# Gate matmuls in two passes of 128 columns that add up in PSUM, and an earlier place for several transfers

## The chip, the cores and the metric

One core of a Trainium2 chip runs the whole block in one launch. The metric is the time on the device in microseconds (us), the median of several runs. The kernel before takes 1783.82 us, the median of 3 runs (1779.32 to 1789.91).

## The reference

One decoder block for 512 tokens of width 1024, in float32: adaLN modulation, a mixer (differential attention beside a gated linear recurrence), and then a PEER layer, which the change is about. PEER scores each token in 8 heads against two sets of 128 keys, keeps the best 16 of each, and picks the 16 best sums; a pair (i1, i2) names one of 128 x 128 experts. For the 8 x 16 chosen experts of a token:

```
q = (h @ w_pq).reshape(B, S, PEER_HEADS, 2, PEER_QHALF)
s = jnp.einsum('bshjd,hjnd->bshjn', q, sub_keys)
v1, i1 = lax.top_k(s[..., 0, :], 16);  v2, i2 = lax.top_k(s[..., 1, :], 16)
cand = v1[..., :, None] + v2[..., None, :]
cidx = i1[..., :, None] * 128 + i2[..., None, :]
top_s, pos = lax.top_k(cand.reshape(..., 256), 16)
gate = softmax(top_s)
a = einsum('tkd,td->tk', expert_u[idx], h)
y = einsum('tk,tkd->td', gate * gelu(a), expert_v[idx])
```

## The kernel before, in words

For 384 of the 512 tokens (SD) the kernel computes every expert densely and multiplies by a gate that is zero where the expert was not chosen; for the other 128 tokens (own rows) it gathers the chosen rows of expert_v and the chosen activations with indirect DMAs on GpSimd. The experts stand in 128 units of 128: a unit of `expert_u` is a tile of 128x1024, multiplied by the transposed activations into a bank of 128x512. All such products are made from float32r halves: a tile is split by ScalarE into a high part (`hi`, Copy to float32r) and by VectorE into the low remainder (`low`), and TensorE runs three passes (high x high, high x low, low x high), 24 matmuls of 512 columns a unit.

The stages from the selection on:
- `stage_select` makes the key scores and, beside the sorting on VectorE, the first 28 units.
- `stage_gates` goes in 48 rounds of 8 tokens (ROUND) and makes one unit (`tile`) in each. The gates of a token are a 128x128 matrix (first index by second index). Its stationary operand is a one-hot of the first indices (`first`, float32r); its moving operand is the one-hot of the second indices weighed by the gate (`weighed`). The gate is split in a high and a low part, h = 0 and 1, that lie side by side, so one matmul of 256 columns per token gives both (line 1829). Four tokens (PER) fill a pair of banks, two such chunks (CHUNKS) a round. ScalarE copies the high halves of a chunk into `gates` (`read_high`, line 1743) and VectorE adds the low halves to them (`add_low`, line 1792). TensorE starts a chunk of the next round when `gates_read` tells that it has been read. The order of the work on each engine is written out in the loop of each engine's block; every 4 rounds SyncE stores a buffer of gates (`store_gates`).
- `stage_rest` makes the last 52 units, keeps 28 of them in memory (`kept`), and weighs each with its gates (`weigh`). SyncE's queue begins with the wait for all stores of the stage before (lines 1890 to 1893), loads two groups of gates, and only then goes on with the unit loads; `store` follows each load six units behind (lines 1898 to 1908). RAW = 4 buffers hold raw units.
- `stage_experts` runs 128 tiles of `expert_v` (18 matmuls each) in an order that mixes tiles whose weighed activations are kept, stored, or plain (to be weighed here); SyncE loads `v_raw`, `acts` and, per group of four plain tiles, `group_gates`. GpSimd gathers own rows (`fetch_row`, line 2154, up to six ahead) and own activations (`fetch_act`, line 2160, one chunk of 16 ahead, on two semaphores); VectorE multiplies a chunk of own activations by the gates (`weigh_own`, line 2250) and adds the rows (`add_row`, line 2260) between its other work, from tile 8 on (`first_row`).

## Time and profile before

| | us |
|---|---|
| median of 3 runs | 1783.82 |
| the profiled execution | 1788.98 |
| its span, first to last instruction | 1787.2 |
| TensorE busy | 1708.3 (96%) |
| VectorE busy | 1311.3 (73%) |
| ScalarE busy | 758.6 (42%) |
| GpSimd busy | 524.9 (29%) |

PE is TensorE's matmuls, PEld its weight loads, DVE VectorE, ACT ScalarE, POOL GpSimd, SP SyncE. Busy times are the union of the records, and records of matmuls overlap: what a matmul costs in a stream is the distance between two starts, not its duration. PEclk and "granted clock" are the share of TensorE's full clock (2.4 GHz) that it was given.

### The profile page before, as it was taken

The page shows a single profiled execution, that of the slowest core. Times are in us where ns is not written, and L with a number is a line of the kernel's source. Part 1 is how long each engine was busy: PE and PEld are TensorE (multiplying, and loading weights), DVE is VectorE, ACT ScalarE, POOL GpSimd, SP SyncE. Part 2 cuts the span into 40 slices and gives each one's busy share as a digit, 9 for nine tenths or more (in the row PEclk, how much of TensorE's full clock was granted, in tenths as well). Part 3 has the DMA queues.
Part 4 walks back from the last instruction along what each step waited for, and adds up shares of the span by engine and source line. Part 5 has one row for each costly group of instructions (what it writes and reads, how often), then busy time and mean ns, then how long its engine had stood idle before and what let it go on. Part 6 is the DMA issues. An engine that isn't in the chain of part 4 may idle for free. (4 is left out here: it accounts for less than half of the span.)

```text
span 1787.2 us, 22493 instructions
## 1 busy us (share of the span) xinstructions
PE 1708.3 (96%) x7869; PEld 1411.2 (79%) x7869; DVE 1311.3 (73%) x2200; ACT 758.6 (42%) x1261; POOL 524.9 (29%) x423
## 2 busy tenths in 40 slices
PE   6999896989999999999998999999999999999997
PEld 5877675778877778888886888888788888888786
DVE  5787776559999969999994333333578868787878
ACT  5225344343322367777773222232333333333333
POOL 1000001115667610000000000000767668667750
PEclk9999998989999999999999999999999999999999
DMA  9563001332144435765667665553898999898985
GB/s 381 214 244 108 1 1 43 147 130 80 62 136 141 139 132 171 217 211 190 204 217 247 214 207 183 176 176 110 307 343 308 329 330 335 314 326 322 335 326 224
DMA packets 160415, 369.96 MB, mean 207 GB/s; under 512 B 16608, under 2 KB 78560, under 8 KB 157024
## 3 DMA queue, kind: packets, MB, share of 16 engines
q1 hardware_dynamic: 137824, 302.08, 48.5%
q0 software_dynamic: 22528, 67.19, 10.7%
q8 instruction: 21, 0.34, 0.1%
q14 instruction: 42, 0.34, 0.1%
HBM read 306.30 MB, written 62.91 MB: 207 GB/s over the span
## 5 line engine op out<-in xcount | busy, mean ns | idle before, releaser
L2022 PE MATMUL banks<-hl,actT 128*128 128x512 f32 x2268 | 518.3, 391 | 7.4 <-DVE actT L2244 7.3
L2022 PEld LDWEIGHTS banks<-hl,actT 128*128 128x128 f32 x2268 | 427.3, 189 | 98.1 <-DVE hl L2239 8.9
L1997 PE MATMUL banks<-actT,hl 128*128 128x512 f32 x1224 | 280.1, 391 | 7.0 <-ACT kept_acts L1931 6.7
L2154 POOL DMA_INDIRECT rows<-in_v,own_index x65 | 86.5, 1331 | 675.0 <-POOLq L1856 608.8
L1814 PE MATMUL banks<-actT,hl 128*128 128x512 f32 x1176 | 275.9, 390 | 1.8 <-PEq L1351 1.8
L1997 PEld LDWEIGHTS banks<-actT,hl 128*128 128x128 f32 x1224 | 231.2, 189 | 56.0 <-issue 7.8
L1814 PEld LDWEIGHTS banks<-actT,hl 128*128 128x128 f32 x1176 | 217.7, 188 | 45.3 <-issue 2.2
L2197 ACT ACTIVATE hl<-v_raw 128x1024 fp32r<-128x1024 f32 x125 | 132.4, 1059 | 273.3 <-PE banks L2022 206.9
L1592 PE MATMUL banks<-actT,hl 128*128 128x512 f32 x1032 | 241.5, 392 | 6.3 <-POOL hl L1439 5.0
L1592 PEld LDWEIGHTS banks<-actT,hl 128*128 128x128 f32 x1032 | 191.5, 188 | 49.6 <-POOL hl L1439 5.9
L2239 DVE TENSOR_TENSOR hl<-v_raw,hl 128x1024 fp32r<-128x1024 f32 x125 | 153.2, 1226 | 77.6 <-ACT hl L2197 57.2
L2160 POOL DMA_INDIRECT rowg<-early_activations,own_at x128 | 175.0, 1367 | 39.1 <-issue 39.1
L1732 ACT ACTIVATE gate_hits<-second_hits,gate_parts 128x128 fp32r<-128x128 bf16 x288 | 125.5, 516 | 68.6 <-DVE second_hits L1772 68.6
L1965 DVE TENSOR_TENSOR kept_acts<-kept_acts,group_gates 128x384 f32<-128x384 f32 x52 | 28.8, 558 | 162.6 <-ACT kept_acts L1931 162.6
L1439 POOL TENSOR_TENSOR hl<-raw,hl 128x1024 fp32r<-128x1024 f32 x42 | 116.5, 2775 | 99.6 <-ACT hl L1453 99.6
L1685 DVE TENSOR_TENSOR gate_hits<-second_hits,gate_parts 128x640 fp32r<-128x640 bf16 x96 | 120.6, 1337 | 0.0
L1931 ACT ACTIVATE kept_acts<-banks 128x512 f32<-128x512 f32 x52 | 31.0, 597 | 192.7 <-PE banks L1997 192.7
L2154 POOL DMA_INDIRECT raw<-in_v,own_index x63 | 83.5, 1325 | 55.8 <-DVE raw L2260 21.9
L217 PE MATMUL banks<-actT,hl 128*128 128x512 f32 x384 | 89.8, 397 | 2.9 <-DVE actT L583 2.9
L217 PEld LDWEIGHTS banks<-actT,hl 128*128 128x128 f32 x384 | 73.8, 193 | 18.5 <-issue 2.9
L1956 DVE TENSOR_TENSOR hl<-raw,hl 128x1024 fp32r<-128x1024 f32 x50 | 61.3, 1227 | 36.1 <-ACT hl L1922 36.1
L716 PE MATMUL banks<-hl,actT 128*128 128x512 f32 x288 | 66.5, 391 | 4.1 <-DVE hl L198 4.1
(274 smaller groups left out, 2173.2 us busy)
## 6 DMA issues: line engine op xcount, KB each, us to landing
raw<-in_u SPq DMA_DIRECT2D x128, 512.0 KB, 3.9
v_raw<-in_v SPq DMA_DIRECT2D x128, 512.0 KB
expert_gates<-gates SPq DMA_DIRECT2D x12, 2048.0 KB, 9.8
group_gates<-expert_gates SPq DMA_DIRECT2D x32, 768.0 KB
wada<-in_w_ada SPq DMA_DIRECT2D x10, 2048.0 KB, 8.3
acts_in<-early_activations SPq DMA_DIRECT2D x100, 192.0 KB
early_activations<-kept_acts SPq DMA_DIRECT2D x52, 256.0 KB, 2.2
early_activations<-gate_acts SPq DMA_DIRECT2D x48, 256.0 KB, 2.3
```

The lines of the kernel that those rows point to most:

```text
L217: last = nc.tensor.matmul(bank[:], hl[:, a, u % m.split, kc * P:(kc + 1) * P], m.actT[:, b, kc, :], start=(kc == 0 and j == 0), stop=(kc = ...
L1439: g.tensor_tensor(hl[:, 1, u, :], raw[:, u, :], hl[:, 0, u, :].bitcast(F32), ALU.subtract).then_inc(m.unit_lo, 1)
L1592: last = nc.tensor.matmul(m.psum[u % 2][:], hl[:, x, u % m.split, kc * P:(kc + 1) * P], m.actT[:, z, kc, :], start=(kc == 0 and j == 0), s ...
L1685: return eng.tensor_tensor(weighed[:, buf, lo:hi, h, :].rearrange("p t k -> p k t"), hits[:, buf, :, lo:hi], part[h][:, n].unsqueeze(1).to ...
L1732: last = A(weighed[:, r % BUFS, u, h, :], hits[:, r % BUFS, :, u], ACT.Copy, scale=part[h][:, at:at + 1])
L1814: last = nc.tensor.matmul(m.psum[n % 2][:], hl[:, x, n % m.split, kc * P:(kc + 1) * P], m.actT[:, z, kc, :], start=(kc == 0 and j == 0), s ...
L1997: last = nc.tensor.matmul(m.psum[u % 2][:], hl[:, x, u % m.split, kc * P:(kc + 1) * P], m.actT[:, z, kc, :], start=(kc == 0 and j == 0), s ...
L2022: last = nc.tensor.matmul(bank(m, t, half)[:], w[:, x, t * P:(t + 1) * P], m.hl[:, z, j, half * S:(half + 1) * S], start=(first and k == 0 ...
L2154: nc.gpsimd.indirect_dma_start(out=fetched[k % FETCH], out_offset=None, in_=rows_of_v, in_offset=bass.IndirectOffsetOnAxis(ap=m.own_index[ ...
L2160: nc.gpsimd.indirect_dma_start(out=own_act[:, k:k + 1], out_offset=None, in_=acts_of_u, in_offset=bass.IndirectOffsetOnAxis(ap=m.own_at[:, ...
L2197: A(v[:, 0, j, :], v_raw[:, j, :], ACT.Copy).then_inc(v_hi, 1)
L2239: V.tensor_tensor(v[:, 1, j, :], v_raw[:, j, :], v[:, 0, j, :].bitcast(F32), ALU.subtract).then_inc(v_lo, 1)
```

## The change

Five things change.

1. A token's gates are made by two matmuls of 128 columns with the same stationary operand, the first with the high part (start) and the second with the low part (stop), so that the sum stands in PSUM. A chunk of four tokens fills one bank instead of two. Chunk 0 is copied out by ScalarE and chunk 1 by VectorE, each once, and each has a semaphore of its own; the addition is gone.
2. In `stage_rest` the wait for the stores of the stage before, and the two gates loads behind it, come after two more unit loads. Stores follow eight units behind instead of six (LATE). The loads of four plain activations, and the first gates that `stage_experts` wants, are issued within the loop instead of after it.
3. The first weighings of `stage_rest` are made at unit 5 instead of 3.
4. In `stage_experts` gathers of own activations run further ahead (`ahead(k)`, up to 8 more), over three semaphores instead of two.
5. Own rows are added from tile 12 on instead of tile 8.

```diff
-        def halves(c):
-            return m.pairs[1 + c][:].rearrange("p (t h j) -> p h j t", t=PER, h=2)
+        def tokens(c):
+            return m.psum[2 + c].rearrange("p (t j) -> p j t", t=PER)
@@ stage_gates, scalar
-                for c in range(CHUNKS):
-                    act.wait_ge(gated, r * CHUNKS + c + 1)
-                    at = r % per_half * ROUND + c * PER
-                    A(gates[:, k, :, at:at + PER], halves(c)[:, 0], ACT.Copy).then_inc(high_read, 1)
+                act.wait_ge(gated, r * CHUNKS + 1)
+                at = r % per_half * ROUND
+                A(gates[:, k, :, at:at + PER], tokens(0), ACT.Copy).then_inc(gates_read[0], 1)
@@ stage_gates, vector
-            def add_low(r):
+            def read_second(r):
                 k = r // per_half % 2
-                for c in range(CHUNKS):
-                    dve.wait_ge(high_read, r * CHUNKS + c + 1)
-                    at = r % per_half * ROUND + c * PER
-                    dst = gates[:, k, :, at:at + PER]
-                    V.tensor_tensor(dst, dst, halves(c)[:, 1], ALU.add).then_inc(gates_read, 1)
+                if r >= 2 * per_half and r % per_half == 0:
+                    dve.wait_ge(stored[k], r // (2 * per_half) * 16)
+                dve.wait_ge(gated, (r + 1) * CHUNKS)
+                at = r % per_half * ROUND + PER
+                V.tensor_copy(gates[:, k, :, at:at + PER], tokens(1)).then_inc(gates_read[1], 1)
@@ stage_gates, tensor
-                        pe.wait_ge(gates_read, i * (per_half * CHUNKS) + ((b - 1) * CHUNKS + c + 1))
+                        pe.wait_ge(gates_read[c], i * per_half + b)
                     for k in range(PER):
                         u = c * PER + k
-                        last = nc.tensor.matmul(m.pairs[1 + c][:, k * 2 * NKEY:(k + 1) * 2 * NKEY], first[:, b % BUFS, u, :],
-                                                weighed[:, b % BUFS, u, :, :].rearrange("p h j -> p (h j)"),
-                                                start=True, stop=True)
+                        for h in range(2):
+                            last = nc.tensor.matmul(m.psum[2 + c][:, k * NKEY:(k + 1) * NKEY], first[:, b % BUFS, u, :],
+                                                    weighed[:, b % BUFS, u, h, :], start=(h == 0), stop=(h == 1))
@@ stage_rest, sync
-            for k in range(2):
-                sp.wait_ge(m.stored[k], 16 * GATE_PAIRS)
-            for u in range(RAW):
-                sp.wait_ge(acts_stored[u], 16 * stored_before)
-            load_gates(0)
-            load_gates(1)
-            for u in range(2):
-                sp.wait_ge(m.early_stored[u], 16 * EARLY // 2)
-            for n in range(RAW, count + RAW + 2):
+            for n in range(RAW, count + LATE):
+                if n == RAW + 2:
+                    for k in range(2):
+                        sp.wait_ge(m.stored[k], 16 * GATE_PAIRS)
+                    for u in range(RAW):
+                        sp.wait_ge(acts_stored[u], 16 * stored_before)
+                    load_gates(0)
+                    load_gates(1)
...
-                if n >= RAW + 2:
-                    store(n - RAW - 2)
+                if n >= LATE:
+                    store(n - LATE)
...
+                if n == count - JG:
+                    for j in range(JG):
+                        sp.dma_start(m.acts_in[:, j, :], a.early[TILES[JG + j], :, 0:SD]
+                                     ).then_inc(m.acts_landed[j], 16)
+                if n - LATE == count - JG - 1:
+                    free = (count // JG - 2) % 2
+                    sp.dma_start(gates[:, free].rearrange("p b j t -> p (b j t)"),
+                                 a.gates[:, SEQUENCE[1][0] * size:(SEQUENCE[1][0] + 1) * size]
+                                 ).then_inc(gates_landed[free], 16)
@@ stage_rest, vector
-                if n == 3:
-                    weigh(0)
-                    weigh(1)
-                if n >= 3:
+                if n == CLEAR:
+                    for k in range(CLEAR - 1):
+                        weigh(k)
+                if n >= CLEAR:
                     weigh(n - 1)
@@ stage_experts
-        first_row = 8
+        first_row = 12
...
+            def ahead(k):
+                return min(SLOTS, k + 1 + CHUNK_K + min(FETCH + 2, k // 2))
...
-                    if c < chunks - 1:
-                        fetch_act(k + CHUNK_K)
+                    for q in range(ahead(k - 1) if k else CHUNK_K, ahead(k)):
+                        fetch_act(q)
```

## Rows read from the trace of the kernel before

**Rows 1.** Busy time and share, and the costliest groups, from the page

```profile
PE 1708.3 (96%) x7869; PEld 1411.2 (79%) x7869; DVE 1311.3 (73%) x2200; ACT 758.6 (42%) x1261; POOL 524.9 (29%) x423
...
L1814 PE MATMUL banks<-actT,hl 128*128 128x512 f32 x1176 | 275.9, 390 | 1.8 <-PEq L1351 1.8
```

**Rows 2.** Busy by stretch: length; PE, PEld, DVE, ACT, POOL (instructions); clock, DMA, GB/s

```profile
720.00:760.00 40.00, 40.00 (x200) 33.98 (x200) 40.00 (x44) 31.57 (x64) 0.00 (x0) 1.00 0.68 212
960.00:1000.00 40.00, 33.29 (x138) 27.08 (x137) 11.54 (x15) 10.10 (x13) 0.00 (x0) 0.91 0.74 250
1240.00:1280.00 40.00, 35.84 (x146) 28.82 (x145) 19.08 (x28) 14.24 (x21) 25.07 (x22) 0.91 0.75 277
1600.00:1700.00 100.00, 98.06 (x433) 80.92 (x433) 80.71 (x95) 36.86 (x50) 75.41 (x51) 1.00 0.90 328
```

**Rows 3.** One round in order of time: start, length (us), engine, line

```profile
761.23 1.27 DVE L1792 TENSOR_TENSOR gates<-gates,banks 128x512 f32<-128x512 f32 x2
...
762.87 1.11 PE L1829 MATMUL banks<-gate_hits,first_hits 128*128 128x256 f32 x8
...
763.82 5.63 PE L1814 MATMUL banks<-actT,hl 128*128 128x512 f32 x24
...
765.31 2.51 DVE L1685 TENSOR_TENSOR gate_hits<-second_hits,gate_parts 128x640 fp32r<-128x640 bf16 x2
...
767.66 1.27 DVE L1792 TENSOR_TENSOR gates<-gates,banks 128x512 f32<-128x512 f32 x2
...
769.29 1.11 PE L1829 MATMUL banks<-gate_hits,first_hits 128*128 128x256 f32 x8
```

**Rows 4.** Groups by line: tiles, shapes, count | busy us, mean ns | idle

```profile
L1829 PE MATMUL banks<-gate_hits,first_hits 128*128 128x256 f32 x384 | 53.6, 282 | 0.1
...
L1829 PEld LDWEIGHTS banks<-gate_hits,first_hits 128*128 128x128 f32 x384 | 52.3, 190 | 4.1 <-issue 0.5
L1743 ACT ACTIVATE gates<-banks 128x512 f32<-128x512 f32 x96 | 51.1, 584 | 0.0
...
L233 DVE COPY projT<-banks 128x512 f32<-128x512 f32 x16 | 11.0, 689 | 11.4 <-PE banks L217 11.4
```

**Rows 5.** TensorE in order of time, two short stretches

```profile
33.24 1.84 PE L277 MATMUL banks<-ones,ada_sums 128*128 128x1 f32 x16
...
387.60 1.05 PE L1605 MATMUL banks<-keys,qT 128*128 128x128 f32 x8
```

**Rows 6.** The weight load of the bf16 matmuls, by line

```profile
L1047 PEld LDWEIGHTS banks<-negmask,ident_bf 128*128 128x128 bf16 x32 | 3.0, 95 | 14.0 <-issue 13.1
```

**Rows 7.** Busy by stretch, as rows 2, and TensorE in order of time

```profile
974.00:978.00 4.00, 4.00 (x10) 3.13 (x11) 3.79 (x6) 2.04 (x3) 0.00 (x0) 0.50 0.26 77
...
973.81 6.52 PE L1997 MATMUL banks<-actT,hl 128*128 128x512 f32 x18 [6.71 <-ACT kept_acts L1931]
```

**Rows 8.** SyncE's queue in order of time, entry of the rest stage

```profile
954.05 0.48 SPq L1699 DMA_DIRECT2D expert_gates<-gates  x1
...
965.54 1.00 SPq L1904 DMA_DIRECT2D raw<-in_u  x2
```

**Rows 9.** Waits of TensorE from 950 on: total, times, longest

```profile
PE banks L2022 <- DVE actT L2244: 7.3, 4, 3.2
PE banks L1997 <- ACT kept_acts L1931: 6.7, 1, 6.7
```

**Rows 10.** In order of time, the start of the experts stage

```profile
1247.69 0.33 SPq L2127 DMA_DIRECT2D group_gates<-expert_gates  x1
...
1257.18 0.56 DVE L2232 TENSOR_TENSOR slotsT<-acts_in,group_gates 128x384 f32<-128x384 f32 x1 [6.28 <-DMA group_gates<-expert_gates]
...
1259.49 25.85 PE L2022 MATMUL banks<-hl,actT 128*128 128x512 f32 x101 [3.18 <-DVE actT L2244]
```

**Rows 11.** What line 2250 waited for, and one resumption of TensorE

```profile
  DMA rowg<-early_activations,own_at: 41.3, 8
...
1662.89 3.42 PE L2022 MATMUL banks<-hl,actT 128*128 128x512 f32 x14 [1.94 <-DVE actT L2244]
```

More of the change, by code:

```diff
@@ L1696, in store_gates @@
                 p, k = divmod(q, 2)
-                sp.wait_ge(gates_read, (q + 1) * per_half * CHUNKS)
+                for c in range(CHUNKS):
+                    sp.wait_ge(gates_read[c], (q + 1) * per_half)
                 dst = a.gates[:, 0:NKEY * SD].rearrange("p (g n) -> p g n", n=NTB * JG * TB)
@@ L1734, in scale_rows, with read_first @@
                 last.then_inc(act_rows, 1)
-            def read_high(r):
+            def read_first(r):
                 k = r // per_half % 2
@@ L1748, in _ @@
                     gelu(n - 1)
-                    read_high(n - 1)
+                    read_first(n - 1)
                 hi(n + 2)
@@ L1753, in _ @@
             gelu(count - 1)
-            read_high(count - 1)
+            read_first(count - 1)
         @block.vector
@@ L1797, in _ @@
                 if n >= 1:
-                    add_low(n - 1)
+                    read_second(n - 1)
                 if n + 1 < count:
@@ L1803, in _ @@
                     operands(n + 1)
-            add_low(count - 1)
+            read_second(count - 1)
         @block.tensor
@@ L1849 @@
 CLEAR = 5
+LATE = 8
 MADE = 2
@@ L1888, in store @@
                 sp.dma_start(a.early[WEIGHED_FROM + n], kept[:, n % KEPT, :]).then_inc(acts_stored[n % RAW], 16)
-            for k in range(2):
-                sp.wait_ge(m.stored[k], 16 * GATE_PAIRS)
-            for u in range(RAW):
-                sp.wait_ge(acts_stored[u], 16 * stored_before)
-            load_gates(0)
-            load_gates(1)
-            for u in range(2):
-                sp.wait_ge(m.early_stored[u], 16 * EARLY // 2)
-            for n in range(RAW, count + RAW + 2):
+            for n in range(RAW, count + LATE):
[6 more added lines that the diff above has]
+                    load_gates(1)
+                    for u in range(2):
+                        sp.wait_ge(m.early_stored[u], 16 * EARLY // 2)
                 if n % JG == 1 and 3 <= n // JG < 7:
@@ L1904, in _ @@
                     sp.dma_start(raw[:, n % RAW, :], a.u[WEIGHED_FROM + n]).then_inc(m.unit_landed[n % RAW], 16)
-                if n >= RAW + 2:
-                    store(n - RAW - 2)
+                if n >= LATE:
+                    store(n - LATE)
                 if n % JG == 3 and 2 <= n // JG < count // JG:
                     load_gates(n // JG)
-            for j in range(JG):
-                sp.dma_start(m.acts_in[:, j, :], a.early[TILES[JG + j], :, 0:SD]).then_inc(m.acts_landed[j], 16)
+                if n == count - JG:
[7 more added lines that the diff above has]
+                                 ).then_inc(gates_landed[free], 16)
             for j in range(MADE):
@@ L2071, in stage_experts @@
         fetch_landed = [sem(f"fetch_landed{i}") for i in range(FETCH)]
-        act_landed = [sem("own_act_landed0"), sem("own_act_landed1")]
+        act_landed = [sem(f"own_act_landed{i}") for i in range(3)]
         fetch_read, own_weighed, own_added = sem("fetch_read"), sem("own_weighed"), sem("own_added")
@@ L2093, in loads_before, with gate_buffer @@
             return sum(k != "kept" for k in kinds[:n // JG])
+        def gate_buffer(q):
+            return (rest_groups + q) % 2
         def source(n):
@@ L2123, in load_gates @@
                 q = plain_before(s * JG) // JG
+                b = gate_buffer(q)
                 if q >= 2:
@@ L2126, in load_gates @@
                 at = SEQUENCE[s][0] * size
-                sp.dma_start(gates[:, q % 2].rearrange("p b j t -> p (b j t)"), a.gates[:, at:at + size]
-                             ).then_inc(gates_landed[q % 2], 16)
+                sp.dma_start(gates[:, b].rearrange("p b j t -> p (b j t)"), a.gates[:, at:at + size]
+                             ).then_inc(gates_landed[b], 16)
             for s in range(GROUPS + 1):
-                if s < GROUPS and kinds[s] == "plain":
+                if 2 <= s < GROUPS and kinds[s] == "plain":
                     load_gates(s)
@@ L2226, in weigh @@
                 q = i // JG
+                b = gate_buffer(q)
                 if j == 0:
-                    dve.wait_ge(gates_landed[q % 2], ((rest_groups + 1 - q % 2) // 2 + q // 2 + 1) * 16)
+                    dve.wait_ge(gates_landed[b], ((rest_groups + 1 - b) // 2 + q // 2 + 1) * 16)
                 dve.wait_ge(acts_landed[j], (loads_before(n) + 1) * 16)
@@ L2232, in weigh @@
                 V.tensor_tensor(weighed[:, i % 3, :].rearrange("p (b t) -> p b t", t=TB),
-                                acts[:, j, :].rearrange("p (b t) -> p b t", t=TB), gates[:, q % 2, :, j, :],
+                                acts[:, j, :].rearrange("p (b t) -> p b t", t=TB), gates[:, b, :, j, :],
                                 ALU.mult).then_inc(weighed_done, 1)
```

6 lines of the change are left out of this document (3 added, 3 removed).

## The prediction

> **What bounds the kernel now.** I read the page's busy times first: TensorE has work for 96% of the span, VectorE 73%, ScalarE 42% [rows 1]. So a change pays only where it shortens TensorE's queue or closes one of its holes. Then the busy times by stretch: in the gates stage (about 647 to 955 us) TensorE and VectorE are both busy for 40.00 of 40 us at full granted clock; around 960 to 1000 and 1240 to 1280 TensorE has holes and a granted clock of 0.91 [rows 2].
>
> Two engines at 100% leave open which one sets the pace, so I took one round of the stage in order of time. TensorE's small matmuls start at 762.87, the unit's big ones at 763.82, the next small ones at 769.29 [rows 3]. So 8 matmuls of 256 columns take 0.95 us (0.119 each), a unit's 24 of 512 columns 5.47 us (0.228 each), a round 6.42 us. From the record of the 24 themselves, less the length of one, 0.39 [rows 1], (5.63 - 0.39) / 23 = 0.228: the pitch inside a unit is that of the whole, so nothing is waited for between unit and round. VectorE's round (761.23 to 767.66) is 6.43 us: it is just as full, but its results are early: the two additions end at 762.50, before the small matmuls that overwrite their banks, and the operands of a round are made in the round before (they end at 767.82; matmuls at 769.29). ScalarE has air: it is busy 31.57 of the 40 us [rows 2]. TensorE sets the pace, with VectorE on its heels.
>
> **The gates part: what goes.** Per round of 8 tokens ScalarE read two high halves, 128x512 each, 51.1 us / 96 = 0.53 us; VectorE added two low halves, 1.27 us together [rows 3, 4]. Now ScalarE copies one 128x512 chunk and VectorE the other. An existing VectorE copy of that shape from PSUM takes 0.69 us [rows 4], so VectorE sheds about 0.6 us a round and ScalarE 0.5, 29 and 25 us in all. I price both at nothing: TensorE ran back to back and waits for neither. Were VectorE the pace-setter by a hair, TensorE's own pitch, 0.227 in a later stage (433 in 98.06 busy us [rows 2]), allows with 24 x 0.227 + 8 x 0.119 = 6.40 us at most 0.02 a round, 1 us in the stage.
>
> **What comes.** A token had one matmul of 256 columns (high and low side by side) and gets two of 128 with the same stationary operand, so per round 16 instead of 8, in the stage 768 instead of 384, and each comes with a weight load of its own: in the trace there are as many loads as matmuls, 384 and 384 [rows 4]. The stream of columns is the same, 2048 a round; the loads double. So the question is the pitch of an fp32r matmul of 128 columns, which the trace of before doesn't show. Bounds:
> - Below: columns alone. 512 columns take 0.227 us and 256 take 0.119, which is 0.108 for 256 columns and some 0.012 fixed; 128 would be 0.066 us. 16 x 0.066 = 1.06 us a round against 0.95: +0.1 us, +5 us in the stage.
> - Above: that a narrow fp32r matmul falls back to what plain fp32 costs. The plain key matmuls of 128 columns are recorded as two each, 8 records in 1.05 us [rows 5]; less the length of a short matmul's record, 0.28 [rows 4], that is 0.77 / 7 = 0.110 a record, so 0.220 us a matmul. 16 x 0.220 = 3.52: +2.57 us a round, +123 us.
> - Between: the weight load sets it. Matmuls of a single column against f32 weights, 16 in 1.84 us, have a pitch of (1.84 - 0.28) / 15 = 0.104 us [rows 5], hardly less than at 128 columns. So a float32 load can't be followed by the next in less than about 0.104 to 0.110 us, however few columns stream. That the fp32r load is no quicker is in its record: 190 ns mean [rows 4], where a bf16 load takes 95 [rows 6].
>
> I take 0.120 us, today's pitch at 256 columns, where the columns (0.107) and the load (0.104 to 0.110) are about equal: the nearest row of the same type and weights. A round then costs 16 x 0.120 - 0.95 = +0.97 us, and 48 rounds **+46.5 us**. With 0.110 it is 48 x 0.81 = +39.
>
> The Trainium skill ("TensorE: Matmul & The Clock Gate", "LDWEIGHTS") says a load takes its columns divided by 1.2, 107 ns for 128; the single-column row (0.104) agrees, and by it alone the stage would grow by 48 x (1.71 - 0.95) = 36 us. The same page's isolated gap, N/2.4 + 2.5 ns ("Back-to-back issue gap"), would make 56 ns of 128 columns and the stage 3 us shorter; the single-column row speaks against it for float32 weights.
>
> Waits that this part changes: TensorE now waits per chunk for the engine that copies it. ScalarE copies chunk 0 behind the GELU, VectorE chunk 1 behind the operands of the round before, and both have a whole unit (5.5 us) for it. Behind ScalarE's copy stand the next split and its rows, behind VectorE's the hits, a subtraction and operands, 6.4 - 0.6 = 5.8 us in a round that now lasts 7.4; the slack grows everywhere. VectorE's new wait for the stored buffer is ScalarE's of before.
>
> **The late order of transfers.** This part closes holes. Each is its idle time plus what the halved clock after it costs (granted 0.50 at 974 to 978, that is 1.2 GHz, 10 matmuls in 4 us [rows 7]).
> - Entry of the rest stage. SyncE issues the last gates store at 954.05, waits for it, and only then issues the next unit loads at 965.54 [rows 8]; they keep ScalarE waiting, and its GELU keeps TensorE idle 6.7 us [rows 9]. Then 18 matmuls take 6.52 us [rows 7], where 17 x 0.227 + 0.39 = 4.25: 2.3 us. Now loads 4 and 5 are issued ahead of the wait (their buffers are free by then), and TensorE has units 3 to 5, over 16 us, to cover the store and load 6. What is late next is load 6, queued behind the store and both gates loads: landed by about 973, its unit starts at about 983. Gain 9.0 us.
> - Start of the experts. SyncE issues the first gates load at 1247.69, VectorE gets it at 1257.18 after 6.3 us, and TensorE stands 3.2 us; then 101 matmuls take 25.85 us [rows 10] against 100 x 0.227 + 0.39 = 23.1: 2.8 us. Now that load and four of activations go out within the rest stage. On SyncE's queue they pass in front of the last unit stores, which move back by two steps, and GpSimd's first gathers wait for those; gain 5.9 us (3.18 + 2.75). Deferring four weighings to CLEAR is covered: TensorE waits for no weighing there.
> - In the experts VectorE waits 41.3 us in eight places for the gathered own activations [rows 11], and three of them reach TensorE: 7.3 - 3.2 = 4.1 us [rows 9] (the last of the three is in [rows 11]). The gathers now run up to 8 ahead. GpSimd issues as many as before, only earlier, so its total doesn't grow. The first row is added at tile 12 instead of 8: 128 rows in 116 tiles instead of 120, 3% denser, where VectorE with all its work is busy 80.7 of 100 us [rows 2]: it fits. If it doesn't, the end of the stage shows it.
> Sum 9.0 + 5.9 + 4.1 = 19.0. I expect nine tenths, **-17 us**; at worst it is 0 or costs a few us, DMA being busy 0.75 to 0.9 of the time there.
>
> **Sum.** 1788.98 (the profiled execution; its span is 1787.2) + 46.5 - 17 = 1818.5. The profiled execution lies 5.2 us above the median of the three runs, 1783.82; beside that median the sum is 1813. Forecast: **1813 us, +1.6%**, slower.
>
> **Rivals.**
> 1. *Fallback to the plain fp32 price* (0.220 us). For it: the trace has no fp32r matmul under 256 columns, and all 128-column ones are plain and cost that. Against: the type stays fp32r, and at 256 it streams a column per cycle. Then 1783.8 + 123 - 17 = 1890 us.
> 2. *The load is hidden* (0.066 us). For it: 512 and 256 columns lie on a line, and the second pass has the same weights as the first. Against: the single-column pitch. Then 1783.8 + 5 - 17 = 1772 us, faster. It decides from a pitch of about 0.082 us down, where 48 x (16 p - 0.95) is the 17 us that the late order gives back.
> 3. *The load price, but the late order returns nothing*: the loads moved forward collide with stores and gathers, or own rows in fewer tiles run into the end. For it: DMA shares of 0.75 and 0.74 in the stretches of the two large holes [rows 2]. Then 1783.8 + 46.5 and 0 to 5 more: 1830 to 1835 us.
> 4. *Nothing moves*: a pitch near 0.082 with the late order as forecast, 1784. No row lies there.
>
> **Chances.** Forecast 0.73 (1800 to 1826: 0.110 with the whole 19 is 1804, 0.120 with half of it 1821, the rest is the spread of runs); rival 1 0.14; rival 2 0.05; rival 3 0.06; rival 4 0.02. The range 1798 to 1838 holds the forecast and rival 3, 0.79. What a measurement can tell from no change is about 0.5%, 9 us. Faster: rival 2 and a little, 0.06; same: rival 4 and the low edge, 0.05; slower 0.89.
>
> **What would show it.** Right: 768 records of the gate matmuls at a pitch near 0.12 us, a round of about 7.4 us, VectorE with 1.5 us idle in each, no idle time of TensorE at the entry of the rest stage nor at the start of the experts, granted clock 1.00 in both stretches, no long wait of VectorE for gathered activations. Wrong: 0.07 or 0.22 us of pitch (or two records per pass); a TensorE wait for a chunk's copy; the same holes as before.

## The result and the profile after

The changed kernel takes 1812.74 us, the median of 4 runs (1809.01 to 1817.06), beside 1784.28 us of the kernel before (1779.32 to 1789.91); the measured ratio is 1.014, 95% interval 1.0112 to 1.0167 (the two medians give 1.016). That is slower, by an amount clear of the spread. Its profiled execution has 1809.01 us and a span of 1807.3.

In the gates stage TensorE still runs back to back, and now no other engine does. One round in order of time (start, length, engine, line), against [rows 3]:

```profile
763.39 1.90 PE L1830 MATMUL banks<-gate_hits,first_hits 128*128 128x128 f32 x16
...
765.13 5.71 PE L1814 MATMUL banks<-actT,hl 128*128 128x512 f32 x24
765.39 0.69 DVE L1792 COPY gates<-banks 128x512 f32<-128x512 f32 x1 [1.43 <-PE banks L1830]
...
770.68 1.90 PE L1830 MATMUL banks<-gate_hits,first_hits 128*128 128x128 f32 x16
...
772.61 0.69 DVE L1792 COPY gates<-banks 128x512 f32<-128x512 f32 x1 [1.28 <-PE banks L1830]
```

The 16 narrow matmuls run from 763.39 to 765.13: 1.74 us, 0.109 each, where 8 wide ones took 0.95. The unit's 24 take 5.55 us (765.13 to 770.68) instead of 5.47. The round has grown from 6.42 to 7.29 us (763.39 to 770.68). VectorE, packed before, now stands 1.3 to 1.4 us in each round until the banks are ready. The groups by line, against [rows 4]:

```profile
L1830 PEld LDWEIGHTS banks<-gate_hits,first_hits 128*128 128x128 f32 x768 | 93.0, 191 | 4.1 <-issue 0.5
L1830 PE MATMUL banks<-gate_hits,first_hits 128*128 128x128 f32 x768 | 91.2, 272 | 0.1
...
L1792 DVE COPY gates<-banks 128x512 f32<-128x512 f32 x48 | 33.1, 690 | 64.7 <-PE banks L1830 64.7
...
L1743 ACT ACTIVATE gates<-banks 128x512 f32<-128x512 f32 x48 | 28.7, 597 | 12.1 <-PE banks L1830 12.1
```

Twice the loads of the same mean length (191 ns), half the columns each, and one copy for each of two engines: 33.1 us of VectorE in place of 61.4, 28.7 of ScalarE in place of 51.1. In this stage it bought no time; behind it, it did (see "Looking for the fastest").

Behind the gates stage the holes have closed. TensorE's waits from 945 us on, all of them, against [rows 9]:

```profile
PE banks L2031 <- PEq L1857: 0.5, 1, 0.5
PE banks L2006 <- PEq L1651: 0.3, 1, 0.3
```

and the stretches of [rows 2], with 1000 to 1040 and 1280 to 1320, since the stage borders now come 30 to 40 us later (length, busy of PE, PEld, DVE, ACT, POOL, then the clock):

```profile
720.00:760.00 40.00, 40.00 (x225) 34.62 (x224) 31.92 (x34) 26.42 (x50) 0.00 (x0) 1.00 0.65 197
960.00:1000.00 40.00, 39.68 (x215) 33.86 (x214) 22.95 (x24) 20.09 (x35) 0.00 (x0) 1.00 0.70 216
1000.00:1040.00 40.00, 40.00 (x179) 33.10 (x178) 14.45 (x17) 11.88 (x15) 0.00 (x0) 1.00 0.77 273
1240.00:1280.00 40.00, 39.53 (x175) 32.46 (x174) 12.11 (x15) 11.57 (x17) 0.08 (x1) 1.00 0.26 91
1280.00:1320.00 40.00, 40.00 (x178) 33.06 (x178) 22.21 (x30) 15.75 (x22) 26.94 (x23) 1.00 0.71 263
1600.00:1700.00 100.00, 100.00 (x443) 82.81 (x442) 82.06 (x96) 35.76 (x50) 70.20 (x55) 1.00 0.94 339
```

The clock is 1.00 in each, late in the kernel TensorE is busy for 100.00 of 100 us, and the gathered activations are never waited for; line 2267, which waited 41.3 us before [rows 11], has no wait listed. SyncE's queue at the entry of the rest stage shows why, against [rows 8]:

```profile
991.98 0.37 SPq L1700 DMA_DIRECT2D expert_gates<-gates  x1
997.01 3.42 SPq L1906 DMA_DIRECT2D raw<-in_u  x2
1001.69 0.80 SPq L1884 DMA_DIRECT2D group_gates<-expert_gates  x2
```

Two unit loads stand between the last gates store (991.98) and the end of its wait (1001.69). How the span divides:

| | gates stage, first to last small matmul | from there to the end of the span |
|---|---|---|
| before | 302.6 | 837.3 |
| after | 344.2 | 816.4 |
| difference | +41.6 | -20.9 |

### The profile page after: what moved, and what is told of

Read it like the earlier page. It is cut to its first block and busy times, and to the rows that moved or that the text cites. A ratio compares the mean times of both kernels' runs of the same rounds, so it can differ in the third digit from the quotient of the medians.

```text
span 1807.3 us, 23187 instructions
## 1 busy us (share of the span) xinstructions
PE 1743.7 (96%) x8253; PEld 1447.2 (80%) x8253; DVE 1289.7 (71%) x2152; ACT 744.3 (41%) x1213; POOL 502.6 (28%) x423
## 5 line engine op out<-in xcount | busy, mean ns | idle before, releaser
L2031 PE MATMUL banks<-hl,actT 128*128 128x512 f32 x2268 | 514.2, 389 | 0.0
L2167 POOL DMA_INDIRECT rows<-in_v,own_index x65 | 76.4, 1176 | 715.4 <-POOLq L1857 640.8
L1974 DVE TENSOR_TENSOR kept_acts<-kept_acts,group_gates 128x384 f32<-128x384 f32 x52 | 28.7, 557 | 156.8 <-ACT kept_acts L1940 156.8
L1685 DVE TENSOR_TENSOR gate_hits<-second_hits,gate_parts 128x640 fp32r<-128x640 bf16 x96 | 118.3, 1313 | 0.0
L1830 PEld LDWEIGHTS banks<-gate_hits,first_hits 128*128 128x128 f32 x768 | 93.0, 191 | 4.1 <-issue 0.5
L1830 PE MATMUL banks<-gate_hits,first_hits 128*128 128x128 f32 x768 | 91.2, 272 | 0.1
L2167 POOL DMA_INDIRECT raw<-in_v,own_index x63 | 74.3, 1179 | 58.2 <-DVE raw L2277 33.6
```

Source lines behind the costliest of these rows:

```text
L1685: return eng.tensor_tensor(weighed[:, buf, lo:hi, h, :].rearrange("p t k -> p k t"), hits[:, buf, :, lo:hi], part[h][:, n].unsqueeze(1).to ...
L1830: last = nc.tensor.matmul(m.psum[2 + c][:, k * NKEY:(k + 1) * NKEY], first[:, b % BUFS, u, :], weighed[:, b % BUFS, u, h, :], start=(h == ...
L2031: last = nc.tensor.matmul(bank(m, t, half)[:], w[:, x, t * P:(t + 1) * P], m.hl[:, z, j, half * S:(half + 1) * S], start=(first and k == 0 ...
L2167: nc.gpsimd.indirect_dma_start(out=fetched[k % FETCH], out_offset=None, in_=rows_of_v, in_offset=bass.IndirectOffsetOnAxis(ap=m.own_index[ ...
```

## The experiments

The runs were timed in three groups, each side by side with the kernel before: `gates_alone`, `late_alone`, `narrow64` and `twice256` (median of the kernel before 1785.4 us); `high_only`, `bf16_two`, `entry_back` and `gathers_back` (1787.2); the other four (1783.8). Between groups ratios are compared, not medians. "Gates stage" is the time from the first to the last small matmul of the profiled execution.

### Each half of the change by itself

`gates_alone` is the kernel before with the new `stage_gates`; `late_alone` is the changed kernel with the old one, its reads and additions included:

```diff
@@ late_alone, against the changed kernel, stage_gates
-                        for h in range(2):
-                            last = nc.tensor.matmul(m.psum[2 + c][:, k * NKEY:(k + 1) * NKEY], first[:, b % BUFS, u, :],
-                                                    weighed[:, b % BUFS, u, h, :], start=(h == 0), stop=(h == 1))
+                        last = nc.tensor.matmul(m.pairs[1 + c][:, k * 2 * NKEY:(k + 1) * 2 * NKEY], first[:, b % BUFS, u, :],
+                                                weighed[:, b % BUFS, u, :, :].rearrange("p h j -> p (h j)"),
+                                                start=True, stop=True)
...
```

> The kernel before with the gates part alone: two passes of 128 columns, one copy per chunk; all transfers in the old order. Theory (the weight load sets the pitch of the narrow matmuls, and the two parts of the change are independent): a round of the gates stage lasts 7.28 us as in the changed kernel, 48 rounds x 0.86 = +41 us, and the three kinds of holes (rest entry, start of the experts, gathers) stay: 1784 + 41 = 1825 us, ratio 1.023. Rival (the longer gates stage itself takes away part of the holes, since stores have more time): under 1818 us, and the entry hole of 6.7 us is smaller in the profile.

> The changed kernel with the gates part undone: one matmul of 256 columns per token, read by ScalarE and added by VectorE as before, with the late order of transfers. Theory: no idle time of TensorE after 950 but the two stage borders, 1784 - 20 = 1764 us, ratio 0.989; gates rounds of 6.42 us. Rival (the late order closes the holes only because the longer gates stage gives its stores time): a hole of several us stays at the entry of the rest stage and the time is 1770 or more.

| | median, us | ratio, 95% | gates stage | from there to the end |
|---|---|---|---|---|
| gates_alone | 1819.54 | 1.0174 (1.0122 to 1.0225) | 344.1 | 823.0 |
| late_alone | 1771.95 | 0.9922 (0.9892 to 0.9952) | 302.6 | 817.9 |

The gates stage is what the small matmuls make it, whatever the order of transfers: 302.6 or 344.1. But the two halves aren't independent. `gates_alone` came out at 1819.5, not 1825: beside the new gates part the old order loses less. `late_alone` came out at 1772, not 1764; a hole of 1.3 us stays, less than the "several us" of the rival that forecast 1770 or more, and most of the miss lies in the size of the holes, taken up below. The waits of TensorE in `gates_alone`, and then those of `late_alone`:

```profile
PE banks L2022 <- DVE actT L2244: 2.7, 2, 2.2
PE banks L1997 <- ACT kept_acts L1931: 2.5, 1, 2.5
```

```profile
PE banks L2006 <- ACT kept_acts L1940: 1.3, 1, 1.3
```

In `gates_alone` the hole at the entry is 2.5 us instead of 6.7 [rows 9], and the granted clock stays at 1.00 from 1012 to 1024, so the 2.3 us of half clock are gone too. In the experts stage TensorE waits 2.7 us instead of 7.3, 2.2 of them at the start, and there too the clock stays at 1.00 (1298 to 1310), where the prediction had counted 2.8 us for it. That is 4.2 + 2.3 + 4.6 + 2.8 = 13.9 of the 14.3 us between 837.3 and 823.0. VectorE still waits 38.6 us for gathered activations, in eight places, but only 0.6 of it reaches TensorE instead of 4.1; why was not followed up. For the entry SyncE's queue tells more:

```profile
988.50 5.81 SPq L1705 DMA_DIRECT2D raw<-in_u  x1
...
996.80 0.37 SPq L1700 DMA_DIRECT2D expert_gates<-gates  x1
...
1007.31 1.67 SPq L1904 DMA_DIRECT2D raw<-in_u  x3
```

and that of the kernel before, ahead of what [rows 8] shows of it:

```profile
946.88 5.83 SPq L1704 DMA_DIRECT2D raw<-in_u  x1
```

In `gates_alone` the last small matmul starts at 995.7 and the last gates store is issued at 996.80, 1.1 us later. Before, it was 949.9 and 954.05, 4.2 us later [rows 8]: SyncE was still held up by a unit load whose issue takes 5.83 us behind the store of 2 MB ahead of it. In `gates_alone` that hold-up (988.50 to 994.3) is over as the last round begins (994.10). So the unit loads behind the wait go out 11.6 us after the last small matmul (1007.31) instead of 15.6 (965.54).

The rival named for `gates_alone` gets its smaller hole, though not its time (under 1818). Its reason, the longer stage, is not the whole of it: `high_only` and `bf16_rows` below keep rounds of 6.4 us and shift SyncE's queue just as far.

### What a narrow matmul costs

```diff
@@ narrow64, against the changed kernel
-                            last = nc.tensor.matmul(m.psum[2 + c][:, k * NKEY:(k + 1) * NKEY], first[:, b % BUFS, u, :],
-                                                    weighed[:, b % BUFS, u, h, :], start=(h == 0), stop=(h == 1))
+                            at = k * NKEY + h * (NKEY // 2)
+                            last = nc.tensor.matmul(m.psum[2 + c][:, at:at + NKEY // 2], first[:, b % BUFS, u, :],
+                                                    weighed[:, b % BUFS, u, 0, h * (NKEY // 2):(h + 1) * (NKEY // 2)],
+                                                    start=True, stop=True)
@@ twice256, against late_alone
+                        for again in range(2):
+                            last = nc.tensor.matmul(m.pairs[1 + c][:, k * 2 * NKEY:(k + 1) * 2 * NKEY],
...
@@ high_only, against the changed kernel
-                        for h in range(2):
+                        for h in range(1):
...
-                                                    weighed[:, b % BUFS, u, h, :], start=(h == 0), stop=(h == 1))
+                                                    weighed[:, b % BUFS, u, h, :], start=True, stop=True)
```

> The changed kernel with each of the 16 gate matmuls of a round cut to 64 columns (the two of a token give the left and the right half of the high part; the low part of the gates is left out). Theory (the float32 weight load sets the pitch): 0.111 us each as at 128 columns, a round 7.28 us, the time that of the changed kernel, 1813 us within 0.3%. Rival (an fp32r pass narrower than 256 columns streams at half rate, two cycles a column): 64 columns take 0.053 + 0.006 = 0.06 us, 16 of them 0.95 instead of 1.8 us, the time 1813 - 41 = 1772 us.

> The kernel with the late order alone, each gate matmul of 256 columns issued twice (the same result written again): 16 loads and 4096 columns a round instead of 8 and 2048. Theory (a load costs about 0.11 us and hides behind 256 columns at best equally long): pitch 0.119 to 0.120 us, a round 6.42 + 0.96 = 7.38 us, 46 us more than the late order alone, that is 5 us slower than the changed kernel though it streams twice its columns: 1810 us. Rival (columns are what costs): the same as the theory gives for this one, but narrow64 then is fast. If VectorE's round of 6.4 us and the bank reads got in the way, the round would be over 7.5 us with waits of TensorE for gates_read.

> The changed kernel without the second pass: 8 fp32r matmuls of 128 columns a round (the low part of the gates is left out). Theory (cost = number of loads x 0.111 us): the small matmuls of a round take 0.89 us, as long as 8 of 256 columns (0.95), a round 6.36 us and the time 3 to 4 us under the late order alone: 1768 us. Rival (the accumulation in PSUM by the second pass is what costs, or the wait for a chunk's copy): then 8 of 128 columns would have a pitch of 0.066 us and a round of 6.0 us: 1752 us.

The small matmuls and the unit after them, in `narrow64`, `twice256` and `high_only`:

```profile
760.53 5.71 PE L1814 MATMUL banks<-actT,hl 128*128 128x512 f32 x24
766.08 1.87 PE L1831 MATMUL banks<-gate_hits,first_hits 128*128 128x64 f32 x16
767.78 5.71 PE L1814 MATMUL banks<-actT,hl 128*128 128x512 f32 x24
```

```profile
765.07 2.08 PE L1830 MATMUL banks<-gate_hits,first_hits 128*128 128x256 f32 x16
766.98 5.63 PE L1814 MATMUL banks<-actT,hl 128*128 128x512 f32 x24
772.45 2.08 PE L1830 MATMUL banks<-gate_hits,first_hits 128*128 128x256 f32 x16
```

```profile
764.77 1.00 PE L1830 MATMUL banks<-gate_hits,first_hits 128*128 128x128 f32 x8
765.61 5.71 PE L1814 MATMUL banks<-actT,hl 128*128 128x512 f32 x24
771.16 1.00 PE L1830 MATMUL banks<-gate_hits,first_hits 128*128 128x128 f32 x8
```

| | matmuls x columns | time of the small ones | each | round | ratio to before, 95% |
|---|---|---|---|---|---|
| high_only | 8 x 128 | 0.84 | 0.105 | 6.39 | 0.9898 (0.9876 to 0.9920) |
| late_alone | 8 x 256 | 0.95 | 0.119 | 6.42 | 0.9922 (0.9892 to 0.9952) |
| narrow64 | 16 x 64 | 1.70 | 0.106 | 7.25 | 1.0143 (1.0092 to 1.0193) |
| changed kernel | 16 x 128 | 1.74 | 0.109 | 7.29 | 1.014 (1.0112 to 1.0167) |
| twice256 | 16 x 256 | 1.91 | 0.119 | 7.38 | 1.0161 (1.0112 to 1.0211) |

With the number of matmuls fixed at 16, a quarter of the columns (64 against 256) saves 0.21 us in the small matmuls and 0.13 in the round; with the columns of each fixed at 128, half of the matmuls saves 0.90 in both. The times were 1811.63 us for `narrow64` (expected 1813), 1815.34 for `twice256` (1810) and 1768.29 for `high_only` (1768). `narrow64` separates the two readings of 0.11 us at 128 columns: at half rate 64 columns would take 0.06 us, and they take 0.106. The accumulation in PSUM isn't the cost either: `narrow64` has none and is no faster.

### The type of the weights

`bf16_two` is the changed kernel with both operands in bf16 (`rounded` is a bf16 buffer); `bf16_rows` turns the loop of VectorE's weighing around, so that it writes neighbouring values and steps in what it reads:

```diff
@@ bf16_two, against the changed kernel
-        first = sb("first_hits", [P, BUFS, ROUND, NKEY], F32R)
-        weighed = sb("gate_hits", [P, BUFS, ROUND, 2, NKEY], F32R)
+        first = sb("first_hits", [P, BUFS, ROUND, NKEY], BF16)
+        weighed = sb("gate_hits", [P, BUFS, ROUND, 2, NKEY], BF16)
...
-            m.dve.then(dve, V.tensor_copy(parts[:, 0, :], slotsT[:, 2, :]))
+            m.dve.then(dve, V.tensor_copy(rounded[:], slotsT[:, 2, :]))
+            m.dve.then(dve, V.tensor_copy(parts[:, 0, :], rounded[:]))
...
@@ bf16_rows, against bf16_two
-                weighed[:, buf, lo:hi, h, :].rearrange("p t k -> p k t"), hits[:, buf, :, lo:hi],
-                part[h][:, n].unsqueeze(1).to_broadcast([P, NKEY, hi - lo]), ALU.mult)
+                weighed[:, buf, lo:hi, h, :], hits[:, buf, :, lo:hi].rearrange("p k t -> p t k"),
+                part[h][:, n].unsqueeze(2).to_broadcast([P, hi - lo, NKEY]), ALU.mult)
```

> The changed kernel with both operands of the gate matmuls in bf16 (the one-hot is exact; the gate is split into a bf16 high and a bf16 low part), still two passes of 128 columns. Theory (what costs is the load of float32 weights): the bf16 load has a record of 95 ns instead of 190, so the pitch falls from 0.111 to between 0.056 (the columns) and 0.08 us; 16 of them take 0.9 to 1.3 us, a round 6.4 to 6.8 us, the time 1770 to 1790 us. Rival (any second instruction per token costs its 0.11 us, whatever the type): 1813 us as the changed kernel.

> bf16_two with VectorE writing the weighed one-hots token by token, so that it writes 128 neighbouring bf16 values and steps in what it reads, instead of the other way round. Theory A (VectorE's writes of single bf16 values 256 values apart were what made its operation 3.2 instead of 1.3 us): at most 1.3 us again, VectorE's round under 6 us, TensorE back to back with 16 x 0.056 + 5.5 = 6.4 us a round: 1765 to 1770 us, at or just under the late order alone (1772). Theory B (bf16 output of this operation is slow in any order): the operation stays near 3.2 us and the time near 1905 us.

`bf16_two` took 1905.10 us, ratio 1.0675 (1.0646 to 1.0704): outside both expectations by a wide margin, though the matmuls became as cheap as the theory said. From its timeline, and the group of the weighing operation:

```profile
761.13 1.14 PE L1832 MATMUL banks<-gate_hits,first_hits 128*128 128x128 bf16 x16 [0.87 <-DVE gate_hits L1686]
...
762.08 5.71 PE L1816 MATMUL banks<-actT,hl 128*128 128x512 f32 x24
...
764.34 5.98 DVE L1686 TENSOR_TENSOR gate_hits<-second_hits,gate_parts 128x640 bf16<-128x640 bf16 x2
```

```profile
L1686 DVE TENSOR_TENSOR gate_hits<-second_hits,gate_parts 128x640 bf16<-128x640 bf16 x96 | 287.9, 3228 | 0.0
...
L1832 PE MATMUL banks<-gate_hits,first_hits 128*128 128x128 bf16 x768 | 64.6, 247 | 100.1 <-DVE gate_hits L1686 100.1
```

The 16 narrow matmuls take 0.95 us (761.13 to 762.08) in this round. But VectorE's operation went from 1313 ns in the changed kernel to 3228 ns, 2 x 1.9 us a round, TensorE waited 100 us for it in all, and between those waits its granted clock fell (0.90 at 800 to 840 us). `bf16_rows` keeps the types and changes only the order of that operation:

```profile
L1686 DVE TENSOR_TENSOR gate_hits<-second_hits,gate_parts 128x640 bf16<-128x640 bf16 x96 | 119.4, 1286 | 0.0
...
L1832 PEld LDWEIGHTS banks<-gate_hits,first_hits 128*128 128x128 bf16 x768 | 43.0, 98 | 13.1 <-issue 12.8 <-DVE gate_hits L1686 0.3
```

```profile
762.53 1.07 PE L1832 MATMUL banks<-gate_hits,first_hits 128*128 128x128 bf16 x16
...
763.41 5.73 PE L1816 MATMUL banks<-actT,hl 128*128 128x512 f32 x24
...
768.98 1.07 PE L1832 MATMUL banks<-gate_hits,first_hits 128*128 128x128 bf16 x16
```

1286 ns, a load record of 98 ns, 16 narrow matmuls in 0.88 us (0.055 each), a round of 6.45 us, and 1771.03 us, ratio 0.9935 (0.9914 to 0.9956). Theory A holds: bf16 by itself costs VectorE nothing here (1286 ns), and float32r written in the old order cost nothing either (1313 ns); only bf16 in the old order does. Reading and writing order were turned together, but the reads of `bf16_two` are those of the changed kernel, so the price is on the side of the writing. With bf16 weights two passes of 128 columns are as cheap as one float32r matmul of 256: the stage takes 303.8 us against 302.6.

### The late order taken apart

Three runs put back one part each in `late_alone`:

```diff
@@ entry_back, stage_rest
-                if n == RAW + 2:
+                if n == RAW:
@@ start_back, stage_rest
-                if n == count - JG:
-                    for j in range(JG):
-                        sp.dma_start(m.acts_in[:, j, :], a.early[TILES[JG + j], :, 0:SD]
-                                     ).then_inc(m.acts_landed[j], 16)
-                if n - LATE == count - JG - 1:
-                    free = (count // JG - 2) % 2
...
+            for j in range(JG):
+                sp.dma_start(m.acts_in[:, j, :], a.early[TILES[JG + j], :, 0:SD]).then_inc(m.acts_landed[j], 16)
...
+            free = (count // JG - 2) % 2
...
@@ gathers_back, stage_experts
-        first_row = 12
+        first_row = 8
...
-                return min(SLOTS, k + 1 + CHUNK_K + min(FETCH + 2, k // 2))
+                return min(SLOTS, k + 1 + CHUNK_K + 0 * k)
```

> The late order alone (gates part undone) with the wait for the stores and the two gates loads back in front of the unit loads of the rest stage. Theory: the hole at the entry comes back, 3 to 7 us idle and up to 2 us of halved clock: 1776 to 1780 us. Rival (the hole of 6.7 us in the profiled execution of before was an unlucky one and is usually covered): within 2 us of 1772.

> The late order alone (gates part undone) with the loads of the four plain activations and of the first gates of the experts stage back behind the loop of the rest stage. Theory: VectorE waits for the gates again at the start of the experts, TensorE stands 2 to 3 us and then runs at the halved clock for some 3 us: 1776 to 1778 us against 1772. Rival (with the border otherwise unchanged the wait is covered): 1772 us.

> The late order alone (gates part undone) with the gathers of own activations back to one chunk of 16 ahead and the own rows back to tile 8. Theory: VectorE waits some 6 us at each chunk again and three or four of these waits reach TensorE, 4 us in all: 1776 us against 1772. Rival (with the other holes closed the tiles have more lead and nothing reaches TensorE): 1772 us.

| | median | ratio, 95% | last small matmul to the end | against late_alone |
|---|---|---|---|---|
| late_alone | 1771.95 | 0.9922 (0.9892 to 0.9952) | 817.9 | |
| entry_back | 1779.16 | 0.9949 (0.9926 to 0.9973) | 825.7 | +7.8 |
| start_back | 1776.26 | 0.9959 (0.9945 to 0.9972) | 821.8 | +3.9 |
| gathers_back | 1774.23 | 0.9927 (0.9903 to 0.9951) | 822.0 | +4.1 |

Waits of TensorE in `entry_back`, `start_back` and `gathers_back`:

```profile
PE banks L2006 <- ACT kept_acts L1940: 6.8, 1, 6.8
```

```profile
PE banks L2028 <- DVE actT L2258: 2.2, 1, 2.2
```

```profile
PE banks L2031 <- DVE actT L2261: 3.2, 3, 2.2
```

Each hole comes back where its part was put back. (In `start_back` the wait at the entry is also 1.9 us instead of 1.3, and the step between the stages 1.4 instead of 0.5; with the 2.2 us that is its 3.9.) The sizes by the profiled executions, 7.8 + 3.9 + 4.1 = 15.8 us, make up most of the 19.4 between before and `late_alone` (837.3 - 817.9); the later stores and the later first weighings were not put back by themselves, and `gathers_back` puts back two things at once. By the ratios the entry is worth about 0.3%, the start 0.4% and the gathers 0.05%, but all three intervals overlap that of `late_alone`: what is shown is where the holes are, and each size only by one profiled execution.

### Looking for the fastest

```diff
@@ late_entry3, against late_alone; bf16_rows_entry, against bf16_rows
-                if n == RAW + 2:
+                if n == RAW + 3:
```

> The late order alone (gates part undone) with the wait for the gates stores one unit load later still. Theory: the 1.3 us at the entry go, 1770 to 1771 us against 1772. Rival: no difference beyond the spread.

> bf16_rows with the wait for the gates stores one unit load later still (unit load 6 goes ahead of it too). Theory: the 1.3 us that TensorE still waits at the entry of the rest stage in the late order alone go: 1 to 2 us under bf16_rows, the fastest version. Rival: the gates loads come so late that the weighing or the next loads fall behind; a hole further on, and no gain.

1771.26 us, ratio 0.9928 (0.9914 to 0.9942), and 1771.78 us, 0.9929 (0.9917 to 0.9942): no gain over `late_alone` or `bf16_rows`. In `late_entry3` the wait at the entry stays. In `bf16_rows_entry` there was none to remove: in `bf16_rows` itself TensorE's longest wait at the entry is 0.3 us, at the stage border, as in the changed kernel. In order of time in `late_entry3`:

```profile
959.56 0.48 SPq L1699 DMA_DIRECT2D expert_gates<-gates  x1
961.42 7.98 SPq L1906 DMA_DIRECT2D raw<-in_u  x3
...
972.56 1.06 ACT L1931 ACTIVATE hl<-raw 128x1024 fp32r<-128x1024 f32 x1 [7.69 <-DMA raw<-in_u]
...
974.24 9.99 PE L2006 MATMUL banks<-actT,hl 128*128 128x512 f32 x43 [1.63 <-ACT kept_acts L1940]
```

So all four versions with the late order and gate matmuls that cost about 0.9 us a round lie at 1771 to 1772 us, some 0.7% under the kernel before, and can't be told apart. The expectation of `late_entry3` looked at the wrong transfer. The last gates store is issued at 959.56, the next unit loads at 961.42, when the stage border has been passed; SyncE is held for 7.98 us in issuing them, and ScalarE waits 7.69 us, to 972.56, for load 4. It is load 4 that is late, behind the store's bytes, not load 6 behind SyncE's wait.

Whether load 4 is late hangs on how far ahead of the border the store goes out. In `high_only`, with rounds just as short, it is 4.3 us instead of 1.9, and TensorE waits there only the 0.3 us of the border:

```profile
952.68 0.44 SPq L1700 DMA_DIRECT2D expert_gates<-gates  x1
957.01 4.96 SPq L1906 DMA_DIRECT2D raw<-in_u  x2
```

The difference begins at ScalarE's GELU of a finished unit, first in the kernel before, then in `high_only`:

```profile
765.66 0.57 ACT L1723 ACTIVATE gate_acts<-banks 128x512 f32<-128x512 f32 x1
```

```profile
764.97 0.60 ACT L1724 ACTIVATE gate_acts<-banks 128x512 f32<-128x512 f32 x1 [1.62 <-PE banks L1814]
```

In the kernel before, the unit ends at 762.87 and its GELU starts 2.8 us later: ScalarE is behind, because in every round it waits 1.4 us for the hits of a VectorE that is itself full. In `high_only` the unit ends at 764.77 and the GELU starts 0.2 us later, after waiting for TensorE. The activations' store, the gates store and the unit load behind them on SyncE's queue follow the GELU. Measured on the last rounds (waits without the 0.3 us of the border itself):

| | round | GELU after its unit | last gates store, after the last round's first small matmul | unit loads, after that store | TensorE's wait there | from the last small matmul to the end |
|---|---|---|---|---|---|---|
| late_alone | 6.42 | 2.8 | 5.0 | 1.9 | 1.3 | 817.9 |
| late_entry3 | 6.42 | 2.8 | 5.0 | 1.9 | 1.6 | 818.2 |
| high_only | 6.39 | 0.2 | 2.5 | 4.3 | none | 816.4 |
| bf16_rows | 6.45 | 0.2 | 2.4 | 4.5 | none | 816.5 |
| changed kernel | 7.29 | 0.2 | 2.7 | 5.0 | none | 816.4 |
| twice256 | 7.38 | 0.2 | 3.5 | 4.4 | none | 816.4 |

So either of two things closes this hole: longer rounds, even with the old reads and additions (`twice256`), or the work taken off ScalarE and VectorE, even with short rounds (`high_only`, `bf16_rows`). It is worth 1.5 us (817.9 to 816.4).

## Why the prediction was right, and where its terms were off

**The bound.** TensorE sets the pace of the gates stage: shown. VectorE and ScalarE lost 28 and 22 us of work there, and the stage grew by 41.6 us, to what the matmuls take. But the step "I price both at nothing" holds for the gates stage alone. ScalarE ran 2.8 us behind TensorE before, and that set when SyncE's last transfers went out; catching up moves them forward by some 2.5 us and closes 1.3 us of hole behind the stage (`high_only` and `bf16_rows` against `late_alone`). Beside the old order it has a part in the 14.3 us that `gates_alone` got back, together with the longer rounds; how they share it was not separated.

**The price of a narrow matmul.** The step was "the weight load sets it", between 0.066 and 0.220 us. Shown by `narrow64` and `twice256` against each other, and by `bf16_rows`, which halves the load's record (191 to 98 ns) and brings the pitch to 0.055. (Both operands changed type there; that the fixed price is the load's, and not another one of a float32r matmul, rests on the load's record.) Rivals 1 and 2, 0.220 and 0.066 us, are ruled out by the measured 0.109. The size was off: I took 0.120, today's pitch at 256 columns, and it is 0.109; the row of the plain narrow matmuls, 0.110 [rows 5], was the better one. 48 x (1.74 - 0.95) is 38 us instead of 46.5.

What was missing in the sum is 0.08 us in the 24 matmuls behind the narrow ones, 5.55 instead of 5.47 us, 4 us in the stage. It is there in every kernel whose small matmuls are narrow, bf16 too (`bf16_rows` 5.57), and in neither with 256 columns. The trace of before had it: behind the narrow plain matmuls of [rows 5] a unit's 24 take 5.54 us.

```profile
388.41 5.70 PE L1592 MATMUL banks<-actT,hl 128*128 128x512 f32 x24
393.95 1.05 PE L1605 MATMUL banks<-keys,qT 128*128 128x128 f32 x8
```

Why is open; that the unit's first loads can't run ahead of so short matmuls is a guess that was not tested. 38 and 4 us together are the measured 41.6, where the prediction had 46.5.

The Trainium skill ("TensorE: Matmul & The Clock Gate", "LDWEIGHTS") gives 107 ns for a load of 128 columns; the pitch of 0.105 to 0.109 us here agrees, while a load's record lasts 191 ns. The isolated gap that this page of the Trainium skill gives for 128 columns, 56 ns, is met too, but only once the operands are bf16 (0.055), and there in a stream where each matmul has its load. Under "Weight-path perf modes" the Trainium skill says that the fast weight load is on when there are 128 weights and the input type is not FP32; it doesn't say how float32r counts, and the halved load record in `bf16_rows` (98 ns) agrees with float32r counting as FP32.

**The late order.** Each of its three holes was where the prediction put it, and in the changed kernel all three closed; load 6 behind the stores was covered, as forecast. With ScalarE late and short rounds it is load 4 that comes late, which the step had not seen. In size, forecast and put back: entry 9.0 and 7.8 us (6.8 of hole against the 1.3 left, and a granted clock of 0.50 from 976 to 980 in `entry_back`), start 5.9 and 3.9 (a hole of 2.2 instead of 3.2, and a clock of 1.00 behind it), gathers 4.1 and 4.1. The prediction took 17 us for all. The medians say 13.4 (1785.4 to 1771.95). The profiled executions say 17.0 by their spans (1787.2 to 1770.2) and 19.4 from the last small matmul on; the gates stage of `late_alone` began 2.5 us later (649.7 against 647.2), ahead of anything that was changed. The holes were read from one execution that itself lay 5 us over its median; I moved the whole sum by those 5 us instead of taking them from the holes. Whether its holes were deeper than usual is not shown, since one execution of each kernel was profiled, and `entry_back` has the same hole again (6.8 us).

**The sum.** I added the two terms. They overlap: +34.1 us for the gates part on the old order (1785.4 to 1819.54), about +41 on the new one (1771.95 to 1812.74); the late order is worth 13.4 us beside the old gates part and about 7 beside the new one (1819.54 to 1812.74; 823.0 - 816.4 = 6.6 in the profiled executions). In the order old, late, both: -13.4 + 40.8 = +27.4 (+28.5 as timed beside the changed kernel, 1784.28 to 1812.74), where the prediction had -17 + 46.5 = +29.5. The forecast of 1813 for a measured 1812.74 is luck in its last digits: one term was 5.7 us too high, the other 3.6 too large the other way. That the holes depend on how SyncE's blocked issue falls against the last round was in no step of it.

**The rest.** No wait of TensorE for a chunk's copy appeared, and own rows from tile 12 on fit: the changed kernel has no wait of TensorE in the experts stage but 0.5 us at its start. Rival 3 is ruled out, since the late order by itself is faster than the kernel before (0.9922, 0.9892 to 0.9952).

## What to carry to other kernels

Count the weight loads before the columns: here a float32r matmul of 64 or 128 columns cost about 0.11 us (0.106, 0.109) and one of 256 hardly more (0.119), so a split that keeps the columns and doubles the matmuls doesn't pay unless each still streams some 256 columns. In bf16 128 columns cost 0.055; fewer were not run. Work taken off engines that TensorE doesn't wait for buys nothing in that stage, even when one of them shows 100% busy, but look at what those engines release: here a late GELU held back SyncE's queue and cost 1.3 us at the next border. A hole priced from one profile is the depth of one execution, and it changes when another part of the kernel changes.

## What the runs showed of the hardware that was not expected

- VectorE's multiplication of 128x640 took 1286 ns writing bf16 values side by side (and stepping in its reads), 3228 ns writing them 256 values apart, and 1313 to 1341 ns writing float32r that way (`bf16_rows`, `bf16_two`, changed kernel, `late_alone`).
- The float32r pitch at 256 columns (0.119) is 0.01 us over the pitch at 128 (0.109) and at 64 (0.106), which are alike.
- A SyncE issue of a unit load behind a 2 MB store took 5.8 us, against 0.43 for others, and where that fell moved the next unit loads by 4 us (15.6 to 11.6 us after the last small matmul) and a hole in the next stage with them (6.7 to 2.5 us; before and `gates_alone`).
- A unit's 24 matmuls of 512 columns took 5.54 to 5.57 us behind matmuls of 128 or 64 columns, plain, float32r or bf16 (the selection stage of before, changed kernel, `narrow64`, `high_only`, `bf16_rows`), and 5.47 behind ones of 256 (the gates stage of before, `twice256`).
